# Two-layer decoder trunk: the gated unit reads its input in token order, x is added to in plain order, and the first half's join goes by 512 tokens

## The reference

```python
def sublayer(x, fn, mod_k, g_pre, g_post, res_weight):
    h = rmsnorm(x, g_pre) * (1.0 + scale) + shift      # scale, shift, gate from c
    y = rmsnorm(fn(h), g_post)
    return x + res_weight * gate * y

def s5_mixer(u, ...):
    ug = u.reshape(bsz, s_len, 64, 16)                  # 64 groups of 16 channels
    bu = einsum('gpn,bsgn->bsgp', b_bar, ug)
    _, states = associative_scan(combine, (a_seq, bu), axis=1)   # complex, along tokens
    y = einsum('gnp,bsgp->bsgn', cmat, states).real + d_skip * u
    g = gelu(y)
    a, b = split(g @ w_glu, 2)
    return a * sigmoid(b)

# layer 1: half-step SwiGLU, s5_mixer, half-step SwiGLU (D = 1024, D_FF = 2816)
```

## Time and profile before

| | us |
|---|---|
| median of the runs | 2448.69 |
| lowest, highest | 2447.6, 2456.56 |
| the profiled execution | 2441.95 |
| its span on the slowest core (core 2) | 2440.4 |
| spans of the eight cores | 2423.6 to 2440.4 |
| mean granted clock of the eight cores | 0.987 to 0.990 |

### The profile page before, as it was taken

How to read it: one execution, slowest core, us unless ns; L and a number is a source line. 1 busy time by engine, 2 the same in 40 slices (tenths; PEclk the granted TensorE clock), 3 DMA queues, 4 the chain that set the end, 5 groups by cost and what they waited for, 6 DMA issues and landing times.

```text
span 2440.4 us, 34487 instructions; the slowest of 8 cores (2423.6 to 2440.4 us)
## 1 busy us (share of the span) xinstructions
PE 2303.0 (94%) x11147; PEld 1058.4 (43%) x11365; DVE 1286.1 (53%) x2367; ACT 1000.5 (41%) x1533; POOL 317.5 (13%) x456
## 2 busy tenths in 40 slices
PE   2899999999889999999999999999998998999997
PEld 0344444444334444444444444444443443444446
DVE  4499355247788462743281125387365882455215
ACT  3534344143784651621171126363376463352111
POOL 0000221012000003100400120002200000210111
PEclk9999999999999999999999999999999998999999
DMA  8776778655546666666754456745668555368532
GB/s 244 164 158 155 153 145 174 152 111 125 152 113 147 139 144 132 139 155 143 135 119 74 69 85 144 171 103 118 117 141 201 107 120 103 62 140 173 104 55 75
DMA packets 143617, 320.94 MB, mean 132 GB/s; under 512 B 54081, under 2 KB 56513, under 8 KB 143442
## 3 DMA queue, kind: packets, MB, share of 16 engines
q0 software_dynamic: 50400, 161.67, 41.1%
q1 hardware_dynamic: 93042, 157.06, 20.6%
HBM read 445.41 MB, written 36.49 MB: 197 GB/s over the span
## 4 chain that ended last, share of the span: by engine, by line
PE 74%; DVE 12%; issue 5%; DMA 3%; SPq 3%; ACT 3%; DVEq 0%; ACTq 0%; POOLq 0%; POOL 0%
PE ps L381 74%; DVE xT_sb L397 6%; SPq L425 3%; DVE HB L397 2%; DMA ring<-win_r 1%; DVE Ureg L397 1%; DVE Ureg L402 1%; DMA xT_sb<-xT 1%; DVE Yreg L402 1%; ACT HB L392 1%; DVE Yreg L397 1%; ACT L392 1%; DVE ring L503 1%; ACT rstd L392 1%; DVEq L244 0%
## 5 line engine op out<-in xcount | busy, mean ns | idle before, releaser
L381 PE MATMUL ps<-HB,ring 128*128 128x512 bf16 x3505 | 805.1, 382 | 24.9 <-DMA HB<-Yd_scr 8.2
L381 PE MATMUL ps<-HA,ring 128*128 128x512 bf16 x3000 | 684.7, 381 | 42.9 <-DMA ring<-win_r 27.1
L381 PE MATMUL ps<-Ureg,ring 128*128 128x512 bf16 x2415 | 544.2, 380 | 5.5 <-DMA ring<-wout_r 2.5
L381 PEld LDWEIGHTS ps<-HB,ring 128*128 128x128 bf16 x3584 | 348.1, 98 | 447.5 <-issue 42.3
L397 DVE TENSOR_TENSOR Ureg<-ps,Ureg 128x512 bf16<-128x512 f32 (+1 forms) x368 | 253.4, 689 | 504.6 <-PE ps L381 449.4
L392 ACT ACTIVATE Ureg<-ps 128x512 bf16<-128x512 f32 (+1 forms) x400 | 237.5, 595 | 596.0 <-PE ps L381 590.1
L381 PEld LDWEIGHTS ps<-HA,ring 128*128 128x128 bf16 x3072 | 298.3, 98 | 399.1 <-issue 50.8
L381 PEld LDWEIGHTS ps<-Ureg,ring 128*128 128x128 bf16 x2464 | 240.6, 98 | 292.6 <-issue 6.0
L392 ACT ACTIVATE Yreg<-ps 128x512 f32<-128x512 f32 (+2 forms) x184 | 105.6, 577 | 461.0 <-PE ps L381 436.5
L425 POOL DMA_DIRECT2D ring<-win_r x176 | 94.0, 534 | 1181.9 <-PE ps L381 1112.5
L397 DVE TENSOR_TENSOR sqt<-ps,Yreg 128x512 bf16<-128x512 f32 (+1 forms) x121 | 79.7, 659 | 310.1 <-ACT Yreg L392 307.7
(11 more groups left out here) (130 smaller groups left out, 1324.0 us busy)
## 6 DMA issues: line engine op xcount, KB each, us to landing
ring<-win_r POOLq DMA_DIRECT2D x176, 512.0 KB, 5.8
ring<-ada_r SPq DMA_DIRECT2D x128, 512.0 KB, 4.2
ring<-wout_r POOLq DMA_DIRECT2D x112, 352.0 KB, 5.2
Xs_scr<-xT_sb SPq DMA_DIRECT2D x24, 512.0 KB, 7.8
xT_sb<-Xs_scr SPq DMA_DIRECT2D x24, 512.0 KB, 5.9
xT_sb<-xT SPq DMA_DIRECT2D x32, 256.0 KB, 9.0
ring<-glu_r POOLq DMA_DIRECT2D x16, 512.0 KB, 5.7
outT<-xT_sb SPq DMA_DIRECT2D x24, 256.0 KB, 7.2
```

Source lines behind the costliest of these rows:

```text
L381: P.op("pe", lambda e: e.matmul(o.ap, l.ap, r.ap, start=start, stop=stop), reads=keys(l, r), writes=keys(o), cost=max(0.8 * l.n, r.n / 2.4 ...
```

## The change

`glu` streams, for block nn, column c from 64 nn to 64 nn + 63 as the outer and plane j as the inner dimension: 8 numbers with a step of 128 bf16 (256 bytes), 64 times. This is token order, so the additions to x have no step and block nn is tokens 512 nn to 512 nn + 511. For half 0 the code then goes block by block: `post_norm`, `pre_stats` and `pre_rstd` of the block (`half_norm`) and `pre_h` of the block; `spill` stands behind both. Half 1 keeps whole-half `post_norm` and `pre_norm`.

```diff
-        def post_norm(s, p, perm=False, store=False, yb=None, blocks=((0, 512, 0), (512, 512, 1))):
+        def post_norm(s, p, store=False, yb=None, blocks=((0, 512, 0), (512, 512, 1))):
...
                     stt(y, y, coefc(s, k), r2[t], ALU.mult, ALU.mult, cls=ncls[0])
-                    if perm:
-                        xv = X.f(p * 32768 + k * 4096 + t // 128 * 4, [[1, 4], [8, 128]])
-                        tt(xv, xv, (yb or Y).f(k * 4096 + t * 4, [[128, 4], [1, 128]]), ALU.add)
-                    else:
-                        xv = x_at(k, p * HS + t, n)
-                        tt(xv, xv, y, ALU.add, cls=ncls[0])
+                    xv = x_at(k, p * HS + t, n)
+                    tt(xv, xv, y, ALU.add, cls=ncls[0])
...
+        def half_norm(s, p, s2, p2, nn, yb=None):
+            post_norm(s, p, yb=yb, blocks=((nn * 512, 512, nn),))
+            pre_stats(s2, p2, nn)
+            pre_rstd(nn)
...
-                            mm(PS(bank), rb(slot, k * 256 + which * 128), H[0].b(k * 2048 + nn * 1024, [[1, 512]]), start=(k == 0), stop=(k == 7))
+                            mm(PS(bank), rb(slot, k * 256 + which * 128), H[0].b(k * 2048 + nn * 128, [[1, 64], [128, 8]]), start=(k == 0), stop=(k == 7))
...
         ssm_in(1)
-        post_norm(4, 0, perm=True, yb=U)
+        for nn in range(2):
+            half_norm(4, 0, 5, 0, nn, yb=U)
+            pre_h(5, 0, nn)
         spill(0)
-        pre_norm(5, 0)
...
-        post_norm(4, 1, perm=True, yb=X)
+        post_norm(4, 1, yb=X)
```

## The result

The changed kernel takes 2772.9 us (median of four, 2768.78 to 2775.53) against 2448.1 us: a ratio of 1.131, 95% interval 1.129 to 1.134, or +325 us. The direction was forecast (0.66 for slower); the size, +104 us, was a third of the measured one. The time lies in the stated range, near the value of rival 2 (2785).

The account below looks back on a forecast made before the run. TensorE, busy 94% of the span, was taken to bound the kernel. Strided matmuls +110.6, low-clock saving -4, additions 0 and join -3 gave +103.6 us, so 2552 us for the median, range 2436 to 2790.

Parts of the forecast that it names:

- rival 2: Gated unit's strided matmuls: a fixed time per line, 1.72 ns and more, +340 us, giving 2785 up to 2822; chance 0.17.
- What bounds the kernel: Whole kernel: TensorE busy 94% of the span, so a matmul that grows is paid in full outside a few gaps.
- The price of a strided column: Gated unit's 512 matmuls: 0.432 us each instead of 0.216, by a ratio of two, +110.6 us; chance 0.40.
- The lower end (no cost): Gated unit's matmuls: lower bound of the stride's price, zero, from a free strided PSUM read on ScalarE.
- Four us saved at the low clock: Gap before second gated unit: some 40 matmuls already at the 1.2 GHz level cover part of the price, -4 us.
- Additions in plain order: Additions to x: 32 fall from 1.092 to 0.703 us, -6.2 us of VectorE per half, worth 0 in the second half.
- The join: First half's join by 512 tokens: TensorE's 14.4 us gap goes but is given back in the second gap; net -3 us.
- the forecast's 2.4: Second half's mixer: starts 2.4 us later, as 16.8 us of work ahead replaces 14.4 us of gap.
- the mixer's loads come late: Second half's mixer: block loads wait for the spill of x, with DMA engines full, so the mixer starts no earlier.
- The rival with -14 us: Join: the mixer's chain moves up with TensorE, so the 14.4 us arrive; 2434 without stride cost, chance 0.05.
- rival 1: Gated unit's strided matmuls: TensorE streams at full rate, no cost, only the join's -3 us left, 2446; chance 0.34.
- rival 3: Gated unit's strided matmuls: a fixed addition of 0.76 to 0.89 ns per element, +200 to +233 us; chance 0.09.

Follow-up runs that it names:

- step sweep: Kernel before, with a different step of the streamed operand (2 to 256 bytes) for each of the gated unit's eight weight tiles; 2686.3 us in one run.
- stride alone: Kernel before with only the gated unit's matmuls streaming eight planes in token order (step 256 bytes); 2775.9 us, ratio 1.132.
- the version with 1.095 us: Changed kernel streaming runs of 64 columns, outputs left in plane order, order put right at the addition to x with a 32-byte step; ratio 0.9991.
- join alone: Changed kernel with the gated unit's old operand of 512 neighbouring columns; ratio 0.9991.
- ordered evacuation: Changed kernel streaming runs of 64 columns, with ScalarE and VectorE putting outputs in token order when they read PSUM; ratio 0.9992.
- the run with 118 matmuls: The ordered evacuation kernel with the schedule's assumed size of the last spill's stores halved (262144), changing only written order; 2444.1 us, ratio 0.9969.
- with 98: The ordered evacuation kernel with the schedule's assumed size of the last spill's stores quartered (131072), changing only written order; ratio 1.0002.

## Why the prediction was right or wrong

**What bounds the kernel:** right. TensorE was full, and the price of a matmul was paid in full, +170.4 us in the first unit.

**The price of a strided column: the step that failed.** "I take the ratio, at two: 0.432 us." It is 0.862 us, the fixed time of rival 2, which had 0.17 of the chance. The rows had said so as well as they could: 1.73 ns on ScalarE and 1.86 on VectorE differ by 7%, the ratios 2.07 and 1.69 by 22%; TensorE has 1.68 ns and a ratio of 4.0. Both are two views of one quantity, and I chose the one that left the engine's own speed in. The argument against rival 2, that TensorE reads half the bytes per element, counts bytes where the runs count visits to a line: the step sweep has 0.226 us at 4 bytes, 0.45 at 8, 0.90 at 16, and 0.86 to 0.92 beyond. The lower end (no cost) rested on a PSUM read, which is free at 32 bytes on ScalarE and at 256 bytes on both engines and says nothing about SBUF.

The Trainium skill (Advanced Engine Details and Errata, section SBUF Cachelines) gives lines of 16 bytes, and the runs agree, for TensorE too. It also says that two hits on a line absorb the latency. That does not hold for TensorE at its full rate: runs of 2 columns cost 0.433 us, and only runs of 4 are all but free (0.22).

**Four us saved at the low clock:** right in kind. The matmul is as long at either level, so what ran at 0.43 us grew by less. But "some 40" at the low level is misread from the mean of 0.74: the first 8 of these 26 us, in the kernel before, hold 20 of the 51 matmuls at a granted clock of 1.00,

```profile
2040.00:2048.00 8.00, 5.05 (x20) 1.61 (x20) 0.69 (x1) 1.88 (x2) 0.53 (x1) 1.00 1.10 199
```

so at most 31 were at the low level. What the gap covered was more than that, since its waits could be filled as well. The sum with the measured price is: 512 x 0.646 = +331 us, and about +5 us in the first unit that I had not counted (33 sums of squares at 0.40 us, +6, less a wait of 1 us that went). The stride alone, from the first unit's start to the end, costs +326 us (median of eight cores, 1015.6 against 689.8), so some 10 us were covered in the second gap. How they split between low clock and waits is not shown. The whole change takes 4 us less than the stride alone in this measure (1011.7).

**Additions in plain order:** right, 0.69 us each, and worth nothing that can be told: the version with 1.095 us is as fast.

**The join:** not contradicted in its sum (-3 us forecast; about -2 by its ratio, which is not told from 0), wrong in its parts. TensorE's gap closed but for 2.3 us of waits and 16 matmuls that came in pairs 0.70 us apart (5.5 us for what takes 3.5, at a granted clock of 1.00). The mixer started 7.1 us later, not 2.4: the forecast's 2.4 left out these waits and pairs, 2.3 + 2.0 us. In return, 19 matmuls fewer stood behind the mixer (62.5 us instead of 71.4), where I had put the gain into VectorE's scans. I had also said that TensorE's wait for the reload would grow above 8.2 us. It shrank, to 6.7 us in the join alone and to 2.6 in the changed kernel: the gain was given back ahead of the mixer and not in the second gap. That the mixer's loads come late was half right. They were asked for 2.4 us later in the changed kernel (DMA share 1.05 from 1850 to 1875 in the join alone), but in the ordered evacuation they lay ready 13 us when TensorE came. There the written order held the mixer, as the run with 118 matmuls shows; with 98 the spill does. The rival with -14 us was rightly kept small.

**Rivals and chances:** rival 1 is out by the experiments; rival 3 (a fixed addition of 0.76 to 0.89 ns) too, TensorE's addition being 1.26 ns. More than half of the chance stood on two prices, none and the ratio, that the runs rule out.

## What to carry to other kernels

Where a price must be carried from one engine to another, compare the absolute times and the ratios over the engines that have it, and take the quantity that agrees; for a stride in SBUF it was the time per line visited (1.68 ns on TensorE, 1.73 on ScalarE, 1.86 on VectorE; the last two at one step each), so the fastest reader loses most. A reordering belongs where it is free: on the stream in runs of at least 8 bf16 columns (at 4 it is 0.22 us against 0.216), and at the evacuation of PSUM. When a gap closes and the time stays, look at what the written order puts ahead of the next chain, and move both; but see that no engine then waits for a transfer ahead of work that others need.

## What the runs showed of the hardware

A matmul of 512 bf16 columns takes 0.216 us for a step of 2 bytes, 0.226 at 4, 0.45 at 8, 0.90 at 16, 0.92 at 32, 0.86 from 64 to 256; and 0.216, 0.22, 0.43, 0.86 us for runs of 8 and more, 4, 2 and 1 columns. At 0.86 us it is the same at the granted clock of 1.00 and of 0.50, and the granted clock was 1.00 up to 1766, 0.50 from 1770 on and for the rest of the slow stream (it began at 1762.3), though TensorE is shown as busy throughout. Reading PSUM with a step of 256 bytes costs ScalarE (594 ns against 597) and VectorE (688 ns against 689) nothing.
